# Down product in three passes with all four units through the ring, and Silu and Sigmoid as single activations

## The chip, the core and the metric

One core of one Trainium2 chip runs the kernel. The metric is the device time of one execution in microseconds (us). PE is the matrix engine, ACT the scalar engine with the activation functions, DVE the vector engine, POOL GpSimd, SP the engine whose queue issues most of the loads. The profile shows one execution of the kernel, taken by the hardware profiler.

## What is computed

The program is one inference step of a transformer trunk in float32: 512 new prompt tokens and 8 x 16 sample tokens, 640 rows of width 1024. As `DEPTH` is 1, it has one layer: a stick-breaking attention (16 heads of 64), and behind it a mixture of experts. The change lies in the second. Cut to what matters:

```python
def _grouped_moe(h, router_w, router_bias, w_gate, w_up, w_down):
    s = jax.nn.sigmoid((t @ router_w).astype(jnp.float32))
    sel = (s + router_bias.astype(jnp.float32)).reshape(-1, N_GROUPS, EXPERTS_PER_GROUP)
...
    for e in range(N_EXPERTS):
        he = jax.nn.silu(t @ w_gate[e]) * (t @ w_up[e])
        out = out + gates[:, e:e + 1] * (he @ w_down[e])
```

There are 16 experts in four groups; each token goes to two experts of one group. `w_gate` and `w_up` are 1024 x 512 for an expert, `w_down` 512 x 1024.

## The kernel before

**Slots.** After attention and the router, each token's row is scattered to its two experts' places in DRAM (`slots_in`). Rows of one expert lie together, in slots of 128 rows. The slot loop goes over these slots: PE's, ACT's, DVE's and SP's instructions each have a loop of their own, `Fori(1, m + 1)` on the three that compute (PE, ACT, DVE), and they meet through semaphores. In the runs shown m is 16, so there are 16 rounds; 18 slots in all, of which the first and the last two are partly or wholly outside the loop.

**Three passes of rounded halves.** A product of two float32 matrices is made with three matmuls. Each operand is split into a rounded half, `hi` (type fp32r, made by an ACT `Copy`), and the rest, `lo` (the raw value less `hi`, made by a DVE subtraction); PE adds hi·hi, hi·lo and lo·hi in one accumulation (`acc`, L1184). For the weights, a unit is 128 x 1024 values: `hi_unit` (L533, its instruction L535) writes `w_hi`, `lo_unit` (L537, L539) writes `w_lo`. Both are rings of `RING` = 4 units. A unit's place in the ring comes free when PE has used the unit that was there, which PE tells by `unit_used`; DVE tells PE by `lo_ready` that a unit is whole. A gate or an up matrix is four units, a down matrix too, but of the down matrix only the first `KS` = 3 go through the ring. Its fourth quarter goes to PE as it lies in memory, unrounded (`split_out`, the second `for k`). So a slot has `WUNITS` = 11 units. `units_before(j)` is the count of units ahead of slot j's gate.

**One round, by engine.** The order is written out by hand, and each engine goes through its list.
- PE (`phase_b_pe`, the loop at its end): `half_in(j, 0)`, the gate product, 24 matmuls; `turn_hid(j - 1)` and `next_slot(j)`, transposes of the last slot's hidden rows and of the next slot's x (L1282); `half_in(j, 1)`, the up product, 24; `split_out(j)`, the down product of slot j - 1, 18 in three passes and 2 x 1 unrounded (4 instructions).
- ACT: a `Sigmoid` of a 128 x 1 dummy (L790); `this_up(j)`, four units and the sigmoid of the gate product (L744); `last_down(j)`, the rounded half of `hidT` (L751) and three down units; `next_x_hi(j)` (L761); `next_gate(j)`, four units of the next slot's gate; `keep_y(j - 1)`, which copies the down product out of PE's accumulators (L779) and issues its store to `slots_out` (L782). Before units of a new matrix ACT looks up in a table (`slot_expert`, `slot_fetched`, L543 and L546) which of two buffers holds the expert's weights and how many loads must have landed.
- DVE: four up units; `keep_split_hidT`, a copy of the last quarter of `hidT` (L1018) and the rest of three quarters (L1019); `gate_by_sig`, the sigmoid times the gate product, which makes silu (L1030); three down units; `keep_hid` (L1036); `keep_slotT` (L996), the rest of the next slot's x; four gate units of the next slot.
- SP: the load of the next expert's gate, of the next slot's x, of the up, and of the down weights (L516), each when its buffer is free. The three weight loads are 2 MB each, double-buffered by the expert's parity, and left out when the next slot has the same expert. The down load waits for `down_ready`, which PE signals behind the unrounded quarter. The last down load is made in two parts (`load_down`, L518).

The copy `keep_y` waits for `down_ready` too. The gate units in `next_gate` wait for the down units whose places they take, the fourth for the third down unit, `min(u + 1, KS)`. The last two slots' down products (`out(m)` and `out(m + 1)`) are unrounded matmuls.

**Router.** ACT makes exp(-x) of the logits (L706), DVE adds 1 (L900) and takes the reciprocal (L901), and adds the bias (L902).

**End.** Behind the loop the last two slots are finished, while POOL gathers finished rows of `slots_out` and DVE weighs and adds them (L1069).

Of the kernel before, what the change touches and what calls it, by code (L numbers as in the profile page):

```python
# [17 lines left out]
P = 128  # L18
D = 1024
# [31 lines left out]
def build(nc, io, ctx):  # L51
# [163 lines left out]
    sb("h2_tok_end", [P, NT * D - 2 * D - 2 * FE - KF * P - NT * P])  # L215
# [4 lines left out]
    KS = 3  # L220
    WUNITS = 2 * RING + KS
# [23 lines left out]

    hidT_hi = nc.alloc_sbuf_tensor_at("hidT_hi", [P, KS, P], F32R, offset=tmp_at, align_bytes=32)
    hidT_lo = nc.alloc_sbuf_tensor_at("hidT_lo", [P, KS, P], F32R, offset=tmp_at + 4 * KS * P, align_bytes=32)
# [100 lines left out]
    last_down_loaded = sem("last_down_loaded")  # L348
# [41 lines left out]
    sig_step = sem("sig_step")  # L390
# [28 lines left out]
    def phase_b_sync(sp):  # L419
# [55 lines left out]
        with sp.Fori(1, m) as j:  # L475
# [6 lines left out]
            sp.wait_ge(down_ready, j)  # L482
            sp.nop(nofuse=True)
# [5 lines left out]
        sp.wait_ge(lo_ready, units_before(m) + 2 * RING + KS)  # L489
        sp.nop(nofuse=True)  # L490
        sp.wait_ge(exp_loaded[2], 16 * (m + 1))
        sp.nop(nofuse=True)
        load_down(sp, *before, range(0, KS), exp_loaded[2])
        sp.wait_ge(down_ready, m)
        sp.nop(nofuse=True)
        load_down(sp, *before, range(KS, KF), last_down_loaded)
# [21 lines left out]
    def load_down(sp, e, cond, ks, done):  # L518

        dst = exp_w[:, bass.ds(e % 2, 1), 8192 + ks[0] * D:8192 + ks[0] * D + len(ks) * D].rearrange("p b (k f) -> p b k f", f=D)  # L520
        src = io["exp_w_down"][0].rearrange("e (p k) f -> p e k f", p=P)
        sp.dma_start(dst, src[:, bass.ds(e, 1), ks[0]:ks[0] + len(ks)], cond=cond).then_inc(done, 16)

    def units_before(j):


        return 0 if isinstance(j, int) and j == 0 else j * WUNITS - KS
# [115 lines left out]
    def phase_b_act(act):  # L643
# [62 lines left out]
        act.activation(s_e[:, :, :], fill_ps[:, 0, 0:NT * NE].rearrange("p (t e) -> p t e", e=NE), ACT.Exp,  # L706
                       scale=-1.0).then_inc(sig_exp, 1)
# [20 lines left out]
        def this_up(j):  # L728
# [15 lines left out]
            act.activation(sig[:, :], zb(0), ACT.Sigmoid).then_inc(gate_sig, 1)  # L744

        def last_down(j):
# [17 lines left out]
        def next_gate(j, us=range(RING)):  # L764
# [31 lines left out]
        act.wait_ge(table_set, m + 2)  # L796
        act.activation(zero_a[:, :], eps1[:, :], ACT.Sigmoid).then_inc(table_set, 1)
        b = slot_expert(act, m + 1) % 2
        act.wait_ge(exp_loaded[1], slot_fetched(act, m + 1))
        for u in range(RING):  # L800
            act.wait_ge(unit_used, units_before(m + 1) + u + 1)
            hi_unit(act, b, RING + u)
            if u == 1:
                keep_y(m)
        act.wait_ge(unit_used, units_before(m + 1) + RING)
        act.wait_ge(hid_ready, m + 2)
        act.activation(sig[:, :], zb(0), ACT.Sigmoid).then_inc(gate_sig, 1)
        act.wait_ge(pick_turned, 1)
        act.activation(last_pick_T[:, :], turned_pick, ACT.Copy).then_inc(pick_kept, 1)
        act.wait_ge(table_set, m + 3)  # L810
# [1238 lines left out]
```

## Time and profile before

| what | value |
|---|---|
| median of 3 runs | 837.45 us (837.45, 835.5, 837.93) |
| profiled execution, its span | 832.8 us, 13544 instructions |
| PE busy | 775.9 us (93%) |
| PE weight loads busy (beside PE) | 585.2 us (70%) |
| DVE busy | 576.6 us (69%) |
| ACT busy | 480.0 us (58%) |
| POOL busy | 102.3 us (12%) |
| HBM, read and written | 272 GB/s over the span |

The span reaches from the first to the last instruction of the one execution that was profiled; of that execution the page gives the span and no other time. The times of the runs are device times of other executions, which the profiler didn't watch. The busy shares are means over the whole span; attention, the router and the slot loop have limits of their own, and the loop runs from some 487 us to 764 us of the span.

### The profile page before, as it was taken

The page shows a single profiled execution, that of the slowest core. Times are in us where ns is not written, and L with a number is a line of the kernel's source. Part 1 is how long each engine was busy: PE and PEld are TensorE (multiplying, and loading weights), DVE is VectorE, ACT ScalarE, POOL GpSimd, SP SyncE. Part 2 cuts the span into 40 slices and gives each one's busy share as a digit, 9 for nine tenths or more (in the row PEclk, how much of TensorE's full clock was granted, in tenths as well). Part 3 has the DMA queues.
Part 4 walks back from the last instruction along what each step waited for, and adds up shares of the span by engine and source line. Part 5 has one row for each costly group of instructions (what it writes and reads, how often), then busy time and mean ns, then how long its engine had stood idle before and what let it go on. Part 6 is the DMA issues. An engine that isn't in the chain of part 4 may idle for free.

```text
span 832.8 us, 13544 instructions
## 1 busy us (share of the span) xinstructions
PE 775.9 (93%) x4196; PEld 585.2 (70%) x4197; DVE 576.6 (69%) x720; ACT 480.0 (58%) x540; POOL 102.3 (12%) x165
## 2 busy tenths in 40 slices
PE   2799999999999999689997899999999999999987
PEld 0477878777787878458873577787777777877642
DVE  1375555647474655675567798788888887888697
ACT  5334553645453546571434577777777777777513
POOL 3000202011111112021001670000000000000150
PEclk9989999999999999989997999999999999999999
DMA  8937193939576684541009889758999999998563
GB/s 317 347 122 250 36 338 116 350 100 323 129 280 184 225 232 178 205 157 30 1 20 409 345 361 369 295 198 321 371 391 390 399 407 385 388 395 353 198 206 152
DMA packets 94971, 213.85 MB, mean 257 GB/s; under 512 B 4634, under 2 KB 55898, under 8 KB 88803
## 3 DMA queue, kind: packets, MB, share of 16 engines
q1 hardware_dynamic: 89620, 194.16, 64.3%
q0 software_dynamic: 2880, 10.49, 3.5%
q10 hardware_dynamic: 2448, 8.91, 2.6%
q8 instruction: 13, 0.21, 0.1%
q14 instruction: 10, 0.08, 0.0%
HBM read 181.56 MB, written 44.56 MB: 272 GB/s over the span
## 4 chain that ended last, share of the span: by engine, by line
PE 80%; DVE 7%; DMA 6%; ACT 3%; issue 2%; SPq 2%; POOL 1%; ACTq 0%; DVEq 0%; POOLq 0%
PE z L1184 38%; PE fill_ps L1911 18%; PE z L1911 11%; PE z L1148 5%; DMA ada_w<-in_ada_w 2%; PE z L1282 2%; PE fill_ps L1828 2%; DMA ada_w<-in_sb_w_o 2%; PE fill_ps L1184 1%; SPq L1445 1%; PE fill_ps L1834 1%; PE fill_ps L1315 1%; DVE w_lo L539 1%; DMA w_pair<-in_sb_w_qkv 1%; DVE h_T L1673 1%
## 5 line engine op out<-in xcount | busy, mean ns | idle before, releaser
L539 DVE TENSOR_TENSOR w_lo<-exp_w,w_hi 128x1024 fp32r<-128x1024 f32 x192 | 223.6, 1223 | 48.5 <-ACT w_hi L535 48.4
L535 ACT ACTIVATE w_hi<-exp_w 128x1024 fp32r (+1 forms) x192 | 196.4, 1055 | 57.1 <-PE z L1184 43.4
L1184 PE MATMUL z<-w_hi,x_slotT_hi 128*128 128x512 f32 x288 | 121.9, 423 | 2.8 <-ACT x_slotT_hi L761 1.3
L1184 PE MATMUL z<-w_lo,x_slotT_hi 128*128 128x512 f32 x288 | 113.4, 394 | 0.0
L1184 PE MATMUL z<-w_hi,x_slotT_lo 128*128 128x512 f32 x288 | 90.7, 396 | 0.1
L1911 PE MATMUL fill_ps<-h_hi,wp_hi 128*128 128x512 f32 x192 | 77.8, 405 | 1.7 <-DVE h_lo L1679 1.7
L1911 PE MATMUL fill_ps<-h_lo,wp_hi 128*128 128x512 f32 x192 | 77.1, 401 | 0.0
L1911 PE MATMUL fill_ps<-h_hi,wp_lo 128*128 128x512 f32 x192 | 76.6, 399 | 0.0
L1184 PEld LDWEIGHTS z<-w_hi,x_slotT_hi 128*128 128x128 f32 x288 | 54.2, 188 | 19.3 <-issue 3.8
L1184 PEld LDWEIGHTS z<-w_lo,x_slotT_hi 128*128 128x128 f32 x288 | 54.2, 188 | 14.9 <-issue 3.8
L1184 PEld LDWEIGHTS z<-w_hi,x_slotT_lo 128*128 128x128 f32 x288 | 53.9, 188 | 13.4 <-DVE x_slotT_lo L976 0.5
L1184 PE MATMUL z<-exp_w,hidT 128*128 x96 | 45.8, 611 | 1.0 <-DVE hidT L1025 1.0
L1828 PE MATMUL fill_ps<-ada_w,c_T 128*32 128x512 f32 x192 | 28.2, 714 | 19.5 <-DMA ada_w<-in_ada_w 18.5
L1911 PEld LDWEIGHTS fill_ps<-h_hi,wp_hi 128*128 128x128 f32 x192 | 36.6, 191 | 12.9 <-DVE h_lo L1679 3.2
L621 POOL DMA_INDIRECT exp_w<-slots_out,fetch_i x5 | 7.8, 1564 | 296.8 <-DVE w_lo L539 289.0
L1531 POOL TENSOR_SCALAR_AFFINE_SELECT ew_sp<-ew_sp 128x384 f32<-128x384 f32 (+3 forms) x32 | 14.1, 464 | 237.9 <-DVE ew_sp L1759 237.9
L1911 PEld LDWEIGHTS fill_ps<-h_hi,wp_lo 128*128 128x128 f32 x192 | 36.6, 191 | 8.5
L1911 PEld LDWEIGHTS fill_ps<-h_lo,wp_hi 128*128 128x128 f32 x192 | 36.7, 191 | 7.6
L1594 ACT ACTIVATE ew_t<-ew_t 128x1536 f32<-128x1536 f32 x16 | 23.8, 1488 | 31.5 <-DVE ew_t L1748 31.5
L1573 ACT ACTIVATE wp_hi<-w_pair 128x1024 fp32r<-128x1024 f32 x24 | 24.7, 1056 | 28.5 <-DMA w_pair<-in_sb_w_qkv 28.4
L1600 ACT ACTIVATE sp_hi<-ew_sp 128x1536 fp32r<-128x1536 f32 x16 | 23.8, 1489 | 29.8 <-POOL ew_sp L1546 19.0
L1184 PE MATMUL z<-w_hi,hidT_hi 128*128 128x512 f32 x96 | 38.2, 398 | 0.0
(349 smaller groups left out, 1499.6 us busy)
## 6 DMA issues: line engine op xcount, KB each, us to landing
exp_w<-in_exp_w_gate SPq DMA_DIRECT2D x18, 2048.0 KB
exp_w<-in_exp_w_up SPq DMA_DIRECT2D x18, 2048.0 KB
exp_w<-in_exp_w_down SPq DMA_DIRECT2D x17, 2048.0 KB
ada_w<-in_ada_w SPq DMA_DIRECT2D x12, 2048.0 KB, 10.1
slots_in<-zeros SPq DMA_DIRECT2D x7, 2048.0 KB, 12.8
w_pair<-in_sb_w_qkv SPq DMA_DIRECT2D x24, 512.0 KB, 5.3
slots_out<-y_slot ACTq DMA_DIRECT2D x17, 512.0 KB, 10.4
x_slot<-slots_in SPq DMA_DIRECT2D x16, 512.0 KB, 9.3
```

The lines of the kernel that those rows point to most:

```text
L535: act.activation(w_hi[:, u % RING, :].unsqueeze(1), raw_unit(b, u), ACT.Copy).then_inc(hi_ready, 1)
L539: dve.tensor_tensor(w_lo[:, u % RING, :].unsqueeze(1), raw_unit(b, u), w_hi[:, u % RING, :].bitcast(F32).unsqueeze(1), ALU.subtract).then_ ...
L1148: return pe.matmul(proj_ps(q), lhsT, rhs, start=start, stop=stop, skip_group_check=True)
L1184: return pe.matmul(out, lhsT, rhs, start=start, stop=stop, skip_group_check=True)
L1282: mm = pe.transpose(z[:, 2048 + k * P:2048 + (k + 1) * P], src[:, :].rearrange("p (c k) -> p k c", k=KD)[:, k, :], ident[:, :])
L1315: mm = pe.transpose(fill_ps[:, 0, k * P:(k + 1) * P], hid[:, :].rearrange("p (c k) -> p k c", k=KF)[:, k, :], ident[:, :])
L1531: last = pool.affine_select(out=v, in_=v, compare_op=ALU.is_gt, fill=0.0, base=0, pattern=[[0, n], [1, P]] if n > 1 else [[1, P]], channel ...
L1573: act.activation(wp_hi[:, c], w_pair[:, c], ACT.Copy).then_inc(wp_hi_ready, 1)
L1594: act.activation(ew_t[:, a], ew_t[:, a], ACT.Exp, scale=-1.0).then_inc(exp_ready, 1)
L1600: act.activation(sp_hi[:, a], ew_sp[:, a], ACT.Copy).then_inc(sp_hi_ready, 1)
L1828: mm = pe.matmul(out[CW * g:CW * g + CW, :], c_T[:, k, :], src[:, k, :], start=(k < NG4), stop=(k >= NG4), skip_group_check=True)
L1911: return pe.matmul(out, lhsT, rhs, start=start, stop=stop, skip_group_check=True)
```

## The change

The fourth quarter of the down matrix goes through the ring as well: `KS` is gone, `WUNITS` is 12, `hidT_hi` and `hidT_lo` hold all four quarters, and the down product has 24 matmuls of the three-pass kind and no unrounded one. The fourth gate unit on ACT waits for the fourth down unit in place of the third, and `keep_y` waits for `unit_used` of that unit, with `down_ready` left to the last two slots. The load of the next down weights on SP waits for `lo_ready` of the fourth unit, in place of PE's `down_ready`; the last one is a single load. `Silu` on ACT takes the place of the sigmoid and DVE's product (`gate_by_sig`), `Sigmoid` in the router that of exp, the addition and the reciprocal. The dummy activations go, but for one that asks for `Sigmoid` ahead of the router; `preload_act_table` asks for Silu's table ahead of the loop and for Sqrt's at the end.

```diff
     RING = 4
     UK = KD // RING
-    KS = 3
-    WUNITS = 2 * RING + KS
+    WUNITS = 3 * RING
...
@@ SP's loop
             sp.wait_ge(lo_ready, units_before(j) + 2 * RING)
             fetch_over(1, j, *now)
-            sp.wait_ge(down_ready, j)
-            sp.nop(nofuse=True)
+            sp.wait_ge(lo_ready, units_before(j) + 3 * RING)
             fetch_over(2, j - 1, *before)
         before = next_of(m, -1)
-        sp.wait_ge(lo_ready, units_before(m) + 2 * RING + KS)
...
-        load_down(sp, *before, range(KS, KF), last_down_loaded)
+        sp.wait_ge(lo_ready, units_before(m) + 3 * RING)
+        fetch_over(2, m - 1, *before)
...
@@ ACT, router
-        act.activation(zero_a[:, :], eps1[:, :], ACT.Exp).then_inc(table_set, 1)
+        act.activation(zero_a[:, :], eps1[:, :], ACT.Sigmoid).then_inc(table_set, 1)
...
-        act.activation(s_e[:, :, :], fill_ps[:, 0, 0:NT * NE].rearrange("p (t e) -> p t e", e=NE), ACT.Exp,
-                       scale=-1.0).then_inc(sig_exp, 1)
+        act.activation(s_e[:, :, :], fill_ps[:, 0, 0:NT * NE].rearrange("p (t e) -> p t e", e=NE),
+                       ACT.Sigmoid).then_inc(sig_exp, 1)
...
         m = act.value_load(slot_tab[0:1, TAB_N:TAB_N + 1], min_val=NE - 2, max_val=MAX_SLOTS - 2)
+        act.preload_act_table(ACT.Silu)
         act.wait_ge(table_set, 1)
-        act.activation(zero_a[:, :], eps1[:, :], ACT.Sigmoid).then_inc(table_set, 1)
-        act.wait_ge(table_set, 2)
...
@@ ACT, slot loop
-            act.activation(sig[:, :], zb(0), ACT.Sigmoid).then_inc(gate_sig, 1)
+            act.activation(sig[:, :], zb(0), ACT.Silu).then_inc(gate_sig, 1)
...
-            act.activation(hidT_hi[:, :, :], fill_ps[:, 0, 0:KS * P].rearrange("p (k c) -> p k c", c=P),
+            act.activation(hidT_hi[:, :, :], fill_ps[:, 0, :].rearrange("p (k c) -> p k c", c=P),
                            ACT.Copy).then_inc(hidT_hi_ready, 1)
-            for u in range(KS):
+            for u in range(RING):
                 act.wait_ge(unit_used, units_before(j) + RING + u + 1)
                 hi_unit(act, b, 2 * RING + u)
...
-                    act.wait_ge(unit_used, units_before(j) + 2 * RING + min(u + 1, KS))
+                    act.wait_ge(unit_used, units_before(j) + 2 * RING + u + 1)
                 hi_unit(act, b, u)
-        def keep_y(j):
-            act.wait_ge(down_ready, j + 1)
+        def keep_y(j, last=False):
+            if last:
+                act.wait_ge(down_ready, 1)
+            else:
+                act.wait_ge(unit_used, units_before(j + 1) + 3 * RING)
             act.wait_ge(y_slot_stored, 16 * (j + 1))
...
         with act.Fori(1, m + 1) as j:
-            act.wait_ge(table_set, j + 1)
-            act.activation(zero_a[:, :], eps1[:, :], ACT.Sigmoid).then_inc(table_set, 1)
             this_up(j)
...
@@ DVE
-        step(dve.tensor_scalar_add(s_e[:, :, :], s_e[:, :, :], 1.0))
-        step(dve.reciprocal(s_e[:, :, :], s_e[:, :, :]))
...
-            dve.tensor_copy(hidT[:, KS:KF, :], whole[:, KS:KF, :])
-            dve.tensor_tensor(hidT_lo[:, :, :], whole[:, 0:KS, :], hidT_hi[:, :, :].bitcast(F32),
-                              ALU.subtract).then_inc(hidT_kept, 1)
+            dve.tensor_tensor(hidT_lo[:, :, :], fill_ps[:, 0, :].rearrange("p (k c) -> p k c", c=P),
+                              hidT_hi[:, :, :].bitcast(F32), ALU.subtract).then_inc(hidT_kept, 1)
...
             keep_split_hidT(j - 1)
-            gate_by_sig(j)
-            rest_of_down(j, range(KS))
+            rest_of_down(j, range(RING))
             keep_hid(j)
...
@@ PE, split_out
-            b = slot_expert(pe, j - 1) % 2
-            pe.wait_ge(exp_loaded[2], slot_fetched(pe, j - 1))
             pe.wait_ge(y_slot_kept, j)
             pe.wait_ge(hidT_kept, j)
-            for k in range(KS):
+            for k in range(KF):
...
-            for k in range(KS, KF):
-                for c in range(2):
-                    mm = acc(zb(2 + c), hidT[:, k, :],
-                             exp_w[:, bass.ds(b, 1), 8192 + k * D + c * 512:8192 + k * D + (c + 1) * 512], stop=(k == KF - 1))
-            mm.then_inc(down_ready, 1)
...
-            pe.wait_ge(sig_step, j)
+            pe.wait_ge(gate_sig, j)
```

How this moves the instructions is shown at three places, as each engine has them in its program; words in brackets are semaphores that an instruction waits for, ISA and REGISTER_ALU rows are waits and register work.

On PE, the end of the down product in the slot loop (`split_out`), before:

```order
L1184 MATMUL z<-w_hi,hidT_hi 128x512 [waits lo_ready]
L1184 MATMUL z<-w_lo,hidT_hi 128x512
L1184 MATMUL z<-w_hi,hidT_lo 128x512
L1184 MATMUL z<-w_hi,hidT_hi 128x512
L1184 MATMUL z<-w_lo,hidT_hi 128x512
L1184 MATMUL z<-w_hi,hidT_lo 128x512
L1184 ISA
L1184 MATMUL z<-exp_w,hidT 128x512
L1184 ISA
L1184 MATMUL z<-exp_w,hidT 128x512
L1365 ISA
L1365 COMPARE_AND_BRANCH
```

and with the change, from the same third unit on:

```order
L1153 MATMUL z<-w_hi,hidT_hi 128x512
L1153 MATMUL z<-w_lo,hidT_hi 128x512
L1153 MATMUL z<-w_hi,hidT_lo 128x512
L1297 REGISTER_ALU
L1153 MATMUL z<-w_hi,hidT_hi 128x512 [waits lo_ready]
L1153 MATMUL z<-w_lo,hidT_hi 128x512
L1153 MATMUL z<-w_hi,hidT_lo 128x512
L1153 MATMUL z<-w_hi,hidT_hi 128x512
L1153 MATMUL z<-w_lo,hidT_hi 128x512
L1153 MATMUL z<-w_hi,hidT_lo 128x512
L1327 ISA
L1327 COMPARE_AND_BRANCH
```

Behind the third unit the unrounded matmuls on `exp_w` have given way to six matmuls on the ring's fourth unit, with a wait for `lo_ready` of their own.

On ACT, the end of a round, from the third gate unit to the loop's branch, before:

```order
L772 REGISTER_ALU
L535 ISA [waits unit_used]
L535 ACTIVATE w_hi<-exp_w 128x1024
L535 ISA [waits unit_used]
L535 ACTIVATE w_hi<-exp_w 128x1024
L778 REGISTER_ALU [waits down_ready]
L779 ACTIVATE y_slot<-z 128x1024 [waits y_slot_stored]
L782 ISA [waits y_slot_kept]
L782 DMA slots_out<-y_slot 128x1024
L788 ISA
L788 COMPARE_AND_BRANCH
```

and with the change:

```order
L755 REGISTER_ALU
L519 ISA [waits unit_used]
L519 ACTIVATE w_hi<-exp_w 128x1024
L755 REGISTER_ALU
L519 ISA [waits unit_used]
L519 ACTIVATE w_hi<-exp_w 128x1024
L764 REGISTER_ALU [waits unit_used]
L765 ACTIVATE y_slot<-z 128x1024 [waits y_slot_stored]
L768 ISA [waits y_slot_kept]
L768 DMA slots_out<-y_slot 128x1024
L774 ISA
L774 COMPARE_AND_BRANCH
```

A register addition now stands ahead of the fourth gate unit, as that unit waits for a later count of `unit_used` than the third; and the copy of y waits for `unit_used` where `down_ready` stood.

On ACT, the top of the loop, between the branch and the first up unit, before:

```order
L788 UNCONDITIONAL_BRANCH
L788 ISA
L790 ACTIVATE zero_a<-eps 128x1 [waits table_set]
L543 ISA
L543 TENSOR_LOAD slot_tab
L543 ISA x2
L546 ISA
L546 TENSOR_LOAD slot_tab
L546 ISA x2
L737 ISA [waits up_loaded]
```

and with the change:

```order
L774 UNCONDITIONAL_BRANCH
L774 ISA
L527 TENSOR_LOAD slot_tab
L527 ISA x2
L530 ISA
L530 TENSOR_LOAD slot_tab
L530 ISA x2
L720 ISA [waits up_loaded]
```

The dummy activation with its wait is gone, and the two lookups in `slot_tab` follow the branch at once.

## Rows read from the trace of the kernel before

**Rows 1.** The page: its span, and the group of hi·hi matmuls in the down product.

```profile
span 832.8 us, 13544 instructions
...
L1184 PE MATMUL z<-w_hi,hidT_hi 128*128 128x512 f32 x96 | 38.2, 398 | 0.0
```

**Rows 2.** One round by windows: window, PE, PEld, DVE, ACT, POOL busy, clock, DMA, GB/s.

```profile
644.96:663.40 18.44, 18.44 (x83) 14.46 (x83) 15.43 (x17) 14.10 (x17) 0.00 (x0) 1.00 0.97 393
```

**Rows 3.** The chain of waits, transposes of the next slot (start, us, what).

```profile
523.46 0.90 PE z L1282 x8
542.22 0.90 PE z L1282 x8
560.66 0.90 PE z L1282 x8
```

**Rows 4.** Timeline of PE, 657 to 673: start, us, line, operation, tiles, count [idle before].

```profile
659.50 0.40 PE L1184 MATMUL z<-w_hi,hidT_hi 128*128 128x512 f32 x1
...
663.47 0.40 PE L1184 MATMUL z<-w_hi,hidT_lo 128*128 128x512 f32 x1
663.71 1.88 PE L1184 MATMUL z<-exp_w,hidT 128*128 x4
...
665.65 0.40 PE L1184 MATMUL z<-w_lo,x_slotT_hi 128*128 128x512 f32 x1
...
672.29 0.47 PE L1184 MATMUL z<-w_hi,x_slotT_hi 128*128 128x512 f32 x1
```

**Rows 5.** The timeline of ACT in the same stretch.

```profile
663.99 2.01 ACT L535 ACTIVATE w_hi<-exp_w 128x1024 fp32r x2 [0.34 <-PE z L1184]
665.91 1.01 ACT L779 ACTIVATE y_slot<-z 128x1024 f32<-128x1024 f32 x1
...
667.83 0.20 ACT L790 ACTIVATE zero_a<-eps 128x1 f32<-128x1 f32 x1 [0.92 <-ACT y_slot L779]
669.32 3.90 ACT L535 ACTIVATE w_hi<-exp_w 128x1024 fp32r x4 [1.29 <-DMA exp_w<-in_exp_w_up]
```

**Rows 6.** The timeline of DVE in the same stretch.

```profile
657.52 0.68 DVE L1030 TENSOR_TENSOR sig<-sig,z 128x512 f32<-128x512 f32 x1
658.11 3.49 DVE L539 TENSOR_TENSOR w_lo<-exp_w,w_hi 128x1024 fp32r<-128x1024 f32 x3
...
663.25 4.63 DVE L539 TENSOR_TENSOR w_lo<-exp_w,w_hi 128x1024 fp32r<-128x1024 f32 x4
670.61 3.50 DVE L539 TENSOR_TENSOR w_lo<-exp_w,w_hi 128x1024 fp32r<-128x1024 f32 x3 [2.73 <-ACT w_hi L535]
```

**Rows 7.** The timeline of all engines, 573 to 580 us, in one of two longer rounds.

```profile
573.38 1.00 ACT L779 ACTIVATE y_slot<-z 128x1024 f32<-128x1024 f32 x1
...
577.27 3.90 ACT L535 ACTIVATE w_hi<-exp_w 128x1024 fp32r x4 [1.77 <-PE z L1184]
...
578.56 4.63 DVE L539 TENSOR_TENSOR w_lo<-exp_w,w_hi 128x1024 fp32r<-128x1024 f32 x4 [3.35 <-ACT w_hi L535]
...
579.84 0.50 PE L1184 MATMUL z<-w_hi,x_slotT_hi 128*128 128x512 f32 x1
```

**Rows 8.** The timeline of SP's queue, 645 to 650 us.

```profile
647.73 0.34 SPq L516 DMA_DIRECT2D exp_w<-in_exp_w_down  x1
```

**Rows 9.** The timeline of DVE at the router, 443 to 447 us.

```profile
444.13 0.20 DVE L900 TENSOR_SCALAR s_e<-s_e 128x80 f32<-128x80 f32 x1 [3.30 <-ACT s_e L706]
...
445.05 0.24 DVE L902 TENSOR_TENSOR sel<-s_e,router_b 128x80 f32<-128x80 f32 x1
```

**Rows 10.** The timeline of all engines behind the slot loop, from 776 us.

```profile
776.55 1.01 ACT L779 ACTIVATE y_slot<-z 128x1024 f32<-128x1024 f32 x1
...
788.99 1.28 DVE L1069 SCALAR_TENSOR_TENSOR exp_w<-exp_w,gates,gate 128x1024 f32<-128x1024 f32 x1 [4.55 <-DMA exp_w<-slots_out,fetch_i]
...
795.39 0.68 DVE L1036 TENSOR_TENSOR hid<-sig,z 128x512 f32<-128x512 f32 x1
```

**Rows 11.** Groups of instructions by line, tables of ACT in attention (busy us, mean ns).

```profile
L1597 ACT ACT_TABLE_LOAD x8 | 10.3, 1283 | 0.1
```

More of the change, by code:

```diff
@@ L214, in build @@
     last_pick_T = sb("last_pick_T", [P, NT * P])
-    sb("h2_tok_end", [P, NT * D - 2 * D - 2 * FE - KF * P - NT * P])
+    hidT_lo = sb("hidT_lo", [P, KF, P], F32R)
+    sb("h2_tok_end", [P, NT * D - 2 * D - 2 * FE - 2 * KF * P - NT * P])
     x_slotT_hi = sb("x_slotT_hi", [P, KD, P], F32R)
@@ L244, in build @@
     g_ffn = tmp
-    hidT_hi = nc.alloc_sbuf_tensor_at("hidT_hi", [P, KS, P], F32R, offset=tmp_at, align_bytes=32)
-    hidT_lo = nc.alloc_sbuf_tensor_at("hidT_lo", [P, KS, P], F32R, offset=tmp_at + 4 * KS * P, align_bytes=32)
+    hidT_hi = nc.alloc_sbuf_tensor_at("hidT_hi", [P, KF, P], F32R, offset=tmp_at, align_bytes=32)
     ZIN = -(-(MAX_SLOTS + 1) // (NPAIR - 1))
@@ L389, in build @@
     gate_sig = sem("gate_sig")
-    sig_step = sem("sig_step")
     hid_ready = sem("hid_ready")
@@ L481, in phase_b_sync @@
             fetch_over(1, j, *now)
-            sp.wait_ge(down_ready, j)
-            sp.nop(nofuse=True)
+            sp.wait_ge(lo_ready, units_before(j) + 3 * RING)
             fetch_over(2, j - 1, *before)
         before = next_of(m, -1)
-        sp.wait_ge(lo_ready, units_before(m) + 2 * RING + KS)
[L490 to L495, printed above, removed]
-        load_down(sp, *before, range(KS, KF), last_down_loaded)
+        sp.wait_ge(lo_ready, units_before(m) + 3 * RING)
+        fetch_over(2, m - 1, *before)
         sp.wait_ge(x_slot_loaded, 16 * m)
@@ L516, in load_expert @@
         sp.dma_start(dst, src[:, bass.ds(e, 1)], **more).then_inc(exp_loaded[i], 16)
[L518 to L522, printed above, removed]
     def units_before(j):
-        return 0 if isinstance(j, int) and j == 0 else j * WUNITS - KS
+        return 0 if isinstance(j, int) and j == 0 else j * WUNITS - RING
     def raw_unit(b, u):
@@ L795, in phase_b_act @@
             keep_y(j - 1)
-        act.wait_ge(table_set, m + 2)
-        act.activation(zero_a[:, :], eps1[:, :], ACT.Sigmoid).then_inc(table_set, 1)
         b = slot_expert(act, m + 1) % 2
@@ L803, in phase_b_act @@
             if u == 1:
-                keep_y(m)
+                keep_y(m, last=True)
         act.wait_ge(unit_used, units_before(m + 1) + RING)
         act.wait_ge(hid_ready, m + 2)
-        act.activation(sig[:, :], zb(0), ACT.Sigmoid).then_inc(gate_sig, 1)
+        act.activation(sig[:, :], zb(0), ACT.Silu).then_inc(gate_sig, 1)
         act.wait_ge(pick_turned, 1)
         act.activation(last_pick_T[:, :], turned_pick, ACT.Copy).then_inc(pick_kept, 1)
-        act.wait_ge(table_set, m + 3)
-        act.activation(zero_a[:, :], eps1[:, :], ACT.Sqrt).then_inc(table_set, 1)
-        act.wait_ge(down_ready, m + 2)
+        act.preload_act_table(ACT.Sqrt)
+        act.wait_ge(down_ready, 2)
         act.wait_ge(y_slot_stored, 16 * (m + 2))
@@ L1014, in keep_split_hidT @@
         def keep_split_hidT(j):
-            whole = fill_ps[:, 0, :].rearrange("p (k c) -> p k c", c=P)
             dve.wait_ge(hidT_hi_ready, j + 1)
-            dve.tensor_copy(hidT[:, KS:KF, :], whole[:, KS:KF, :])
-            dve.tensor_tensor(hidT_lo[:, :, :], whole[:, 0:KS, :], hidT_hi[:, :, :].bitcast(F32),
-                              ALU.subtract).then_inc(hidT_kept, 1)
+            dve.tensor_tensor(hidT_lo[:, :, :], fill_ps[:, 0, :].rearrange("p (k c) -> p k c", c=P),
+                              hidT_hi[:, :, :].bitcast(F32), ALU.subtract).then_inc(hidT_kept, 1)
         def keep_hidT(j):
@@ L1025, in keep_hidT, with keep_hid @@
             dve.tensor_copy(hidT[:, :, :], fill_ps[:, 0, :].rearrange("p (k c) -> p k c", c=P)).then_inc(hidT_kept, 1)
-        def gate_by_sig(j):
+        def keep_hid(j):
             dve.wait_ge(gate_sig, j + 1)
-            dve.tensor_tensor(sig[:, :], sig[:, :], zb(0), ALU.mult).then_inc(sig_step, 1)
-        def keep_hid(j):
-            dve.wait_ge(sig_step, j + 1)
             dve.wait_ge(unit_used, units_before(j) + 2 * RING)
@@ L1108, in phase_b_dve @@
         dve.wait_ge(x_slot_loaded, 16 * m)
-        dve.wait_ge(down_ready, m + 2)
+        dve.wait_ge(down_ready, 2)
         for c in range(2):
@@ L1334, in split_out @@
                     acc(zb(2 + c), hidT_hi[:, k, :], w_lo[:, k, cols])
-                    mm = acc(zb(2 + c), hidT_lo[:, k, :], w_hi[:, k, cols])
+                    mm = acc(zb(2 + c), hidT_lo[:, k, :], w_hi[:, k, cols], stop=(k == KF - 1))
                 mm.then_inc(unit_used, 1)
-            for k in range(KS, KF):
-                for c in range(2):
-                    mm = acc(zb(2 + c), hidT[:, k, :],
-                             exp_w[:, bass.ds(b, 1), 8192 + k * D + c * 512:8192 + k * D + (c + 1) * 512], stop=(k == KF - 1))
-            mm.then_inc(down_ready, 1)
         def out(j):
@@ L1384, in phase_b_pe @@
         turn_hid(m + 1)
-        pe.wait_ge(last_down_loaded, 16)
         out(m + 1)
```

3 lines of the change are left out of this document (removed).

## The prediction, made before the changed kernel ran

> **What bounds the kernel now.** I read the page first (its span and its groups), then the table by stages, the chain of waits, and the timeline of one round, engine by engine. A round is one turn of the slot loop; PE's three-pass matmuls of the down product come in 96, six for each of three units, so there are 16 rounds [rows 1]. In a round's stretch PE is busy 18.44 of 18.44 us, and the DMA engines are near full as well, share 0.97 [rows 2]. The chain of waits is PE alone through the loop: from one turn of a slot to the next it takes 18.44 us, and 18.76 in two of the rounds [rows 3]. So a round costs what its matmuls cost, as long as ACT and DVE deliver each unit in time. How near they are to being late is read from the timeline. I count from T, the moment at which PE starts the next slot's gate product. The second gate matmul starts at 665.65 and matmuls of this kind stand 0.234 apart (18 of them from 659.50 to 663.71 [rows 4]), so T = 665.42. PE starts the up product at 672.29, T + 6.87 [rows 4]. Its first unit comes by this path: ACT copies y (665.91, T + 0.49), issues its store, branches, looks up two table entries, rounds the first up unit from 669.32, 3.41 after the start of the copy [rows 5]; DVE subtracts from 670.61 for 1.22 us (three take 3.50, so they stand 1.14 apart) [rows 6]. That is 671.83, 0.46 before PE needs it. In a longer round the copy is 3.89 from the unit, and PE starts 0.06 after DVE's end [rows 7]. So ACT has less than half a microsecond to spare where the slots meet.
>
> **The matmuls.** The fourth quarter of the down product takes PE from 663.71 to T, 1.71 us, as unrounded matmuls [rows 4]. Three passes of two column halves are six matmuls at 0.234, 1.40 us. PE saves 0.31 us a round, 5.0 over 16 rounds. A page of the Trainium skill, TensorE: Matmul & The Clock Gate, section "Wait — 56ns, not 53.3ns?", gives about 216 ns from one warm 512-column matmul to the next; by it the six would take 1.30 and the saving would be 6.6 us. The rows show 0.234, and they decide.
>
> **The wait that it brings.** The down product now uses all four places of the ring, so the last gate unit can't be rounded until PE has used the fourth down unit, at T. Before, its place was free with the third, and ACT did it under the unrounded matmuls (it ends the pair that starts at 663.99, and y follows 0.95 after its start, at 665.91 [rows 5]). ACT answers a used unit quickly: the last three-pass matmul starts at 663.47 and lasts 0.40, so ends at 663.87 [rows 4]; ACT starts at 663.99, 0.12 later [rows 5]. With the last matmul now starting at T − 0.23 and ending at T + 0.17, ACT starts that unit at T + 0.29, and y at T + 1.24 in place of T + 0.49. Behind y on ACT are its store, the branch and the up unit. The change takes the little activation at the loop's top away (667.83 [rows 5]). What that gives lies between nothing and the 0.20 that it lasts; I take 0.05, nearer nothing, since ACT idles 0.92 before it and 1.29 behind it: the path runs through the lookups, not through it. So the up unit starts at T + 1.24 + 3.36 = T + 4.60, DVE 1.29 later as now [rows 5, 6], and its end, 1.22 + 0.06 later [rows 6, 7], is T + 7.17. PE could start at T + 6.87. It waits 0.30 us a round, in the 15 rounds that follow a y copy. The gain of 0.31 is given back but for 0.01; only the first round keeps it whole: **−0.5 us for the typical rounds**.
>
> Two rounds now cost 0.31 too much, by lookups that make 3.41 into 3.89 [rows 3, 7]. If they come back, each costs its whole 0.48, 0.34 more for the two together; if they don't, the kernel gains 0.6. SP's own lookups, which follow its issue of the down weights (647.73 [rows 8]), move ahead with it, away from ACT's; but no row proves that the two disturb each other. I take zero, between −0.6 and +0.8 (the other rounds' lookups vary too).
>
> **DVE.** It loses the product with sig (0.59 to the next start [rows 6]) and a small copy, and gains the subtraction of a unit, 1.14, and a quarter of hidT_lo. Its four gate units end at 663.25 + 4.63 = 667.88, and it idles from there to 670.61, 2.7 us [rows 6]: that covers the net half a microsecond. Its order matters once: the rest of x and the first gate unit now stand behind one more unit. Counted from the first up unit at T + 5.89 in steps of 1.14 (four up units, four down), 0.6 twice (hidT_lo and hid) and 1.14 (x), the first gate unit starts at T + 17.35 and ends at T + 18.57, and the next T is at 7.17 + (18.44 − 6.87 − 0.31) = T + 18.43. PE may start its gate product 0.2 late; the up product would then be ready for PE at 0.2 + 6.87 = 7.07 after the next T, still before its first unit at 7.17. Nothing is added.
>
> **The down weights' load** waits for the last subtraction, not for PE: the fourth down unit ends at about T + 15.7, 2.7 before the next T, where the issue now comes 0.75 after T (647.73, against 665.42 − 18.44 = 646.98) [rows 3, 8]. Some 3.5 us earlier, then, for weights that are used a round and more later, so it is worth nothing. That the loads are near full [rows 2] doesn't bind a round that stays at 18.4.
>
> **The router.** Sigmoid on ACT spares DVE an addition and a reciprocal, from 444.13 to 445.05 [rows 9], with PE, the scatter and the first slot behind them: −0.92. The activation itself takes ACT no longer as far as its size goes; a bound for that is nothing to 0.2.
>
> **The end.** The next to last y copy comes 0.75 later, and so do its store and the gather for which DVE waits until 788.99; from there DVE works through to hid at 795.39 [rows 10]. It has the product with sig less (0.59). So hid, PE's last transposes and the last down product come 0.15 later: +0.15, with 0 and 0.75 as the ends.
>
> **Sum.** −0.5 + 0 − 0.92 + 0.15 = −1.3. The profiled execution's span is 832.8 [rows 1]; it becomes 831.5. The median of the three runs is 4.65 above that span, and with the same around it the time is 837.45 − 1.3 = 836.1, say **836.0 us**. That is 0.17% less; a measurement of this kernel can tell about 0.3%, 2.5 us, from no change (834.9 to 840.0).
>
> **The rivals.**
> *PE's gain comes through.* If ACT is not late (the fourth unit's place is seen earlier than I count, or the path from y to the unit is 0.3 shorter), the rounds give 5.0, the two longer ones 0.6, and the router 0.9: 831.0. For it: 0.3 us is all that it needs, and half of it gives 833.5. Against: each piece of the path is a row, and they repeat in the two rounds that I compared (1.29 in both [rows 5 to 7]). Chance 0.18.
> *ACT's path grows: slower.* Place: the stretch between the y copy and the first up unit. Each 0.1 us there costs PE 0.1 in each of 15 rounds, 1.5 us, since no slack is left. From 0.27 us a round on, the kernel is slower than 840.0. If every round is like the longer ones, 3.89 for 3.41 [rows 7], it is 15 × 0.48 = 7.2: 843.2. For it: such rounds are there. Against: two of 15. Chance 0.12.
> *A table load in each round.* Silu is used in the loop, rounded copies are too; if each turn had to load a table, 1.28 us [rows 11] would stand on ACT's path in each of 15 rounds: 836.0 + 19.2 = 855. The order of the changed kernel has one load ahead of the loop and none in it, so I give it 0.02. The page of the Trainium skill on ScalarE activation tables: per-element evaluation and per-set limits, section "Table sets in the compiler and the runtime", says that the back end places the loads block by block, by which a loop's body might get one of its own; by that rule a load could stand there, and the trace of before shows none in the round of rows 5, which has a function with a table too.
>
> **How the numbers follow.** The forecast, ACT's wait in the place of PE's saving, has 0.68, with a range of its own of 834 to 838.5: −0.6 to +0.8 for the lookups, 0 to +0.6 at the end, 0.05 to 0.2 for the dropped activation (up to −2), and runs that differ by 2 us among themselves. Some 0.16 of it falls below 834.9 and almost none above 840. Faster: 0.18 + 0.16 = 0.34. Slower: 0.12 + 0.02 = 0.14. No change that can be told: 0.52. A range of 831.0 to 839.5 leaves out the lower half of the first rival (0.09) and nearly all of the slower cases.
>
> **What would show it.** In the profile after: 24 three-pass matmuls and no unrounded one in a round; the last gate unit on ACT 0.3 after T and y 0.95 behind it; PE's first up matmul at about T + 7.17, with an idle or stretched stretch of 0.3 put down to DVE's w_lo; rounds of 18.4 as before. PE's busy share in the loop, now full, should fall to about 98%. I am wrong if the rounds shrink to 18.13 (ACT is in time), or if they grow past 18.7 (its path is longer). Each other step has its row: no addition and no reciprocal ahead of sel, and no product with sig on DVE.

## The result and the profile after

The changed kernel takes 840.85 us (median of 8 runs, 837.88 to 844.1); the kernel before, run beside it, 835.92 (8 runs, 834.83 to 837.93). The ratio is 1.0059, 95% interval 1.0044 to 1.0075: **slower by 0.6%, 4.9 us**, where I had forecast no change that can be told, and outside my range. It is the rival that I gave 0.12: ACT's path between the copy of y and the first up unit has grown.

The page after: its span, busy times and the three groups of the down product's matmuls.

```profile
span 841.0 us, 13498 instructions
...
PE 776.6 (92%) x4228; PEld 591.4 (70%) x4229; DVE 582.6 (69%) x700; ACT 488.8 (58%) x537; POOL 96.1 (11%) x165
...
L1153 PE MATMUL z<-w_hi,hidT_lo 128*128 128x512 f32 x128 | 50.7, 396 | 0.0
L1153 PE MATMUL z<-w_hi,hidT_hi 128*128 128x512 f32 x128 | 50.7, 396 | 0.0
L1153 PE MATMUL z<-w_lo,hidT_hi 128*128 128x512 f32 x128 | 50.4, 394 | 0.0
...
slots_out<-y_slot ACTq DMA_DIRECT2D x17, 512.0 KB, 6.5
```

The 128 in place of 96 [rows 1] are the fourth unit's matmuls. The last line is the store of y, 6.5 us from issue to landing. The same line of the page before:

```profile
slots_out<-y_slot ACTq DMA_DIRECT2D x17, 512.0 KB, 10.4
```

The store lands sooner now, and that turns out to be the story.

The table by stages, a stretch of 277 us inside the slot loop, of the kernel before and, below it, of the changed one (columns as in [rows 2]):

```profile
487.00:764.00 277.00, 277.00 (x1230) 217.64 (x1229) 232.14 (x240) 211.69 (x240) 7.79 (x6) 1.00 0.91 364
```

```profile
487.00:764.00 277.00, 272.41 (x1236) 218.51 (x1235) 235.09 (x220) 216.68 (x235) 1.92 (x2) 1.00 0.93 362
```

PE had no gap in this stretch; now it has 4.6 us of gaps, at the same granted clock. From the first up product in the loop to the last, 15 rounds, it is 277.24 before and 284.15 after (starts of PE's matmuls): 6.9 us, more than the whole loss.

The chain of waits of the changed kernel where two slots meet, from the copy of y to PE's first up matmul. "ACTq" is ACT's sequencer; L527 and L530 are the two lookups in `slot_tab`, L768 the issue of y's store, "issue" small gaps:

```profile
671.20 1.02 ACT y_slot L765
...
672.42 0.35 ACTq L768
...
673.12 0.27 ACTq L527
...
673.73 0.67 ACTq L530
...
674.91 1.07 ACT w_hi L519
...
676.20 1.24 DVE w_lo L523
...
677.48 0.74 PE z L1153 x2
```

The chain that ran through PE alone before [rows 3] now goes, in nearly every round, through ACT's copy, store, lookups and first up unit, and through DVE. One link is longer than it was: the second lookup, 0.67 us. The view of the instructions that read `slot_tab` has their duration (min/median/max, ns). The same stretch of the kernel before (from 665.9, the copy of rows 5) and of the changed one:

```profile
L543 ACTq TENSOR_LOAD <-slot_tab x1: 287/287/287, 667.9 to 667.9; - x1
L546 ACTq TENSOR_LOAD <-slot_tab x1: 278/278/278, 668.5 to 668.5; - x1
```

```profile
L527 ACTq TENSOR_LOAD <-slot_tab x1: 274/274/274, 673.1 to 673.1; - x1
L530 ACTq TENSOR_LOAD <-slot_tab x1: 669/669/669, 673.7 to 673.7; - x1
```

I went through the 15 rounds that follow a y copy. Before, the second lookup is never over 0.45 us and the first twice, in the two longer rounds. After, the second is over 0.45 in 13 rounds, up to 1.15, the first in 5. From copy to first up unit it is 3.51 on the mean before and 3.86 after.

What differs around them is the order of two transfers. SP issued the down load 0.3 us after the copy's start in the kernel before, with y's store 0.9 behind it; it now issues it 3.5 us ahead of the copy (667.75 against 671.20), 4.7 ahead of the store. The first packets on ACT's queue then move 3.0 to 3.8 us after the copy's start in most rounds, where it had been 4.6 to 5.4. The issues of the down load and of the next gate load, first in the kernel before, then in the changed one:

```profile
666.17 0.34 SPq L516 DMA_DIRECT2D exp_w<-in_exp_w_down  x1
671.22 0.34 SPq L516 DMA_DIRECT2D exp_w<-in_exp_w_gate  x1
```

```profile
667.75 0.34 SPq L506 DMA_DIRECT2D exp_w<-in_exp_w_down  x1
674.02 0.34 SPq L506 DMA_DIRECT2D exp_w<-in_exp_w_gate  x1
```

The two longer rounds of the kernel before fit: the next slot had the same expert, so the down load was left out (its issue is a row of 0.09 us there), next to nothing stood ahead of the store (the up load landed 0.4 to 0.9 after the store's issue), its packets moved 2.1 after the copy, both lookups were longer (0.65 and 0.40, 0.63 and 0.42), and the up unit came 3.89 after the copy [rows 7]. So **theory A**: lookups take long when y's store is being started, and the early down load no longer holds the store back. **Theory B**: the lookups' place alone, 0.08 earlier since the dummy activation is gone.

### The profile page after: what moved, and what is told of

It is laid out like the page before. It is cut to its first block, busy times and chain, and to the rows that moved or that the text cites. A ratio compares the mean times of both kernels' runs of the same rounds, so it can differ in the third digit from the quotient of the medians.

```text
span 841.0 us, 13498 instructions
## 1 busy us (share of the span) xinstructions
PE 776.6 (92%) x4228; PEld 591.4 (70%) x4229; DVE 582.6 (69%) x700; ACT 488.8 (58%) x537; POOL 96.1 (11%) x165
## 4 chain that ended last, share of the span: by engine, by line
PE 70%; DVE 8%; ACT 6%; issue 5%; DMA 4%; ACTq 4%; POOL 2%; SPq 2%; DVEq 0%; POOLq 0%
PE z L1153 29%; PE fill_ps L1872 18%; PE z L1872 11%; PE z L1117 5%; DMA ada_w<-in_ada_w 2%; DVE w_lo L523 2%; ACT w_hi L519 2%; PE fill_ps L1789 2%; ACTq L530 2%; ACT y_slot L765 2%; PE fill_ps L1117 1%; PE fill_ps L1153 1%; SPq L1406 1%; PE fill_ps L1795 1%; POOL slots_in L556 1%
## 5 line engine op out<-in xcount | busy, mean ns | idle before, releaser
L523 DVE TENSOR_TENSOR w_lo<-exp_w,w_hi 128x1024 fp32r<-128x1024 f32 x208 | 241.7, 1223 | 50.6 <-ACT w_hi L519 50.2
L519 ACT ACTIVATE w_hi<-exp_w 128x1024 fp32r (+1 forms) x208 | 211.8, 1055 | 73.0 <-PE z L1153 64.1
L1153 PE MATMUL z<-w_hi,x_slotT_hi 128*128 128x512 f32 x288 | 117.7, 409 | 8.0 <-DVE w_lo L523 5.4
L1153 PE MATMUL z<-w_hi,hidT_lo 128*128 128x512 f32 x128 | 50.7, 396 | 0.0
L1153 PE MATMUL z<-w_hi,hidT_hi 128*128 128x512 f32 x128 | 50.7, 396 | 0.0
L1153 PE MATMUL z<-w_lo,hidT_hi 128*128 128x512 f32 x128 | 50.4, 394 | 0.0
L1789 PE MATMUL fill_ps<-ada_w,c_T 128*32 128x512 f32 x192 | 26.5, 675 | 21.3 <-DMA ada_w<-in_ada_w 20.3
```

The lines of the kernel that those rows point to most:

```text
L519: act.activation(w_hi[:, u % RING, :].unsqueeze(1), raw_unit(b, u), ACT.Copy).then_inc(hi_ready, 1)
L523: dve.tensor_tensor(w_lo[:, u % RING, :].unsqueeze(1), raw_unit(b, u), w_hi[:, u % RING, :].bitcast(F32).unsqueeze(1), ALU.subtract).then_ ...
L1153: return pe.matmul(out, lhsT, rhs, start=start, stop=stop, skip_group_check=True)
L1789: mm = pe.matmul(out[CW * g:CW * g + CW, :], c_T[:, k, :], src[:, k, :], start=(k < NG4), stop=(k >= NG4), skip_group_check=True)
```

## The experiments

**1. The down load back behind PE, in the changed kernel.**

```diff
-            sp.wait_ge(lo_ready, units_before(j) + 3 * RING)
+            sp.wait_ge(unit_used, units_before(j) + 3 * RING)
             fetch_over(2, j - 1, *before)
```

> One line of the changed kernel goes back in kind: SP's load of the next down weights waits until PE has used the fourth down unit (as before), not for the fourth subtraction. Theory A (the order of two transfers): in the changed kernel the down load is issued 3.5 us before the y copy, so nothing stands ahead of y's store, which starts 3.0 to 3.7 us after the copy's start in place of 4.6 to 5.4, and ACT's second table lookup takes 0.4 to 1.0 us in place of 0.28. With the down load back at 0.3 us after the copy, the lookups take 0.28 again, the first up unit comes 3.32 after the copy (3.84 on the mean now), rounds are 18.4 (18.9 now) and the time is about 833 to 835. Theory B (the loop's top): the lookups are longer because the dummy activation ahead of them is gone and they come 0.08 earlier; then nothing changes here: lookups to 1.0, rounds of 18.9, 840.9.

835.96 us, 0.9996 of the kernel before (0.9981 to 1.001): A, though not the 833 to 835 that I expected of it. One wait is the whole loss. The load is now issued 0.54 ahead of the copy and 1.7 ahead of the store, not 0.3 behind the copy as I wrote. Both of ACT's lookups of a round and a lookup of SP's, again from the view by tile:

```profile
L451 SPq TENSOR_LOAD <-slot_tab x2: 262/268/273, 669.8 to 671.6; - x2
L527 ACTq TENSOR_LOAD <-slot_tab x1: 282/282/282, 670.9 to 670.9; - x1
L530 ACTq TENSOR_LOAD <-slot_tab x1: 277/277/277, 671.5 to 671.5; - x1
```

SP's second (671.6) falls on ACT's second, and neither is long, so it is not lookups that hold each other up. Twelve rounds have such lookups (the second takes 0.28 to 0.38), and are 18.39 to 18.50 long (from one up product to the next). The three others are those in which no down load stands ahead of the store: the first, in which it is issued behind it (8.17 from T to the up product in place of 6.87), and the two with the same expert (18.94 and 18.97). That is why it is no better than the kernel before: its 15 rounds take 278.73, 1.5 more than before, and 1.1 of that is in the first.

**2. The dummy activation back.**

```diff
         with act.Fori(1, m + 1) as j:
+            act.wait_ge(table_set, j)
+            act.activation(zero_a[:, :], eps1[:, :], ACT.Silu).then_inc(table_set, 1)
             this_up(j)
```

> The changed kernel with a 128x1 dummy activation (Silu) and its wait at the top of ACT's loop again. Theory A: no better; the second lookup stays at 0.4 to 1.0 us, rounds 18.9 or 0.1 more, 841 to 842. Theory B: the lookups come as late as in the kernel before and take 0.28 each, the first up unit comes 3.41 after the copy, rounds 18.5, some 834 to 835.

843.48 us (1.0086, 1.0067 to 1.0106). The second lookup is over 0.45 in 12 of 15 rounds, the unit comes 3.92 after the copy. B falls.

**3. The copy of y ahead of the fourth gate unit.**

```diff
             act.activation(y_slot[:, :], z[:, 1024:2048], ACT.Copy).then_inc(y_slot_kept, 1)
+            if behind is not None:
+                hi_unit(act, behind, RING - 1)
             act.wait_ge(y_slot_kept, j + 2)
...
-            next_gate(j)
-            keep_y(j - 1)
+            b = next_gate(j, range(RING - 1))
+            keep_y(j - 1, behind=b)
```

> The changed kernel, but on ACT the copy of y is put ahead of the fourth gate unit, which then runs while the store is issued and the lookups are made; both waited for the same signal of PE. If the chain y copy, store, lookups, first up unit is what sets the rounds (both theories of the lookups, and my reading of the trace after), it begins 0.97 earlier: the first up unit is whole at T + 6.4 (by 3.84 from copy to unit) where PE wants it at T + 6.87, and rounds fall from 18.9 to PE's own 18.14, the time to 828 to 831. Rival: DVE's chain or the loads (7.3 MB a round, 405 GB/s at 18.14) set the rounds as well; then they stay at 18.4 or more and the time at 833 or above.

832.09 us (0.995, 0.9932 to 0.9968), between the two: of fifteen rounds nine are 18.25 to 18.30, three 18.36 to 18.39, three 18.61 to 18.72. The path from the copy does set the rounds. The timeline of ACT in a short one:

```profile
664.69 1.03 ACT L766 ACTIVATE y_slot<-z 128x1024 f32<-128x1024 f32 x1 [0.33 <-PE z L1156]
665.61 1.04 ACT L519 ACTIVATE w_hi<-exp_w 128x1024 fp32r x1
665.92 0.35 ACTq L771 DMA_DIRECT2D slots_out<-y_slot  x1
668.44 2.01 ACT L519 ACTIVATE w_hi<-exp_w 128x1024 fp32r x2 [1.78 <-PE z L1156]
```

The store is issued while the gate unit (665.61) runs, and the unit no longer stands ahead of the copy, so its 0.96 is off the path. The lookups come as late behind the copy as in the changed kernel and are still long, DVE's too when it looks up at the same time:

```profile
L527 DVEq TENSOR_LOAD <-slot_tab x1: 705/705/705, 667.2 to 667.2; - x1
L530 ACTq TENSOR_LOAD <-slot_tab x1: 669/669/669, 667.3 to 667.3; - x1
```

Two engines are held up and let go together, so it is no matter of ACT's own.

**4 and 8. The kernel before with a later down load.** Two tries at the converse, to make the kernel before lose in the same way.

```diff
             sp.wait_ge(down_ready, j)
             sp.nop(nofuse=True)
+            sp.wait_ge(y_slot_stored, 16 * (j + 1))
+            sp.nop(nofuse=True)
             fetch_over(2, j - 1, *before)
```

> The kernel before with one wait more on SP: the down load is issued only when y's store has landed, so that the store has no load of the same round ahead of it. Theory A: y's store starts within 2 to 4 us of the copy in every round as it did in the two longer rounds (in which no down load was issued, its expert being there), ACT's lookups take 0.4 to 0.7 in place of 0.28, the up unit is 0.05 late and a round costs 18.7 to 18.8: 13 rounds by 0.32, some 839 to 840. Theory B: no lookup gets longer, rounds of 18.44, 835.9.

863.06 us (1.0314, 1.0285 to 1.0343), for another reason: SP, held up by the store, issues the next loads too late, and PE waits for the next slot's x. The view of waits, 600 to 800 us (us in total, times, longest):

```profile
PE z L1284 <- DMA x_slot<-slots_in: 17.6, 4, 5.2
```

The time tells nothing of A. The trace agrees with it in the two rounds in which no weight load was moving when the store was issued: the first lookup takes 0.70 and 0.65 there. In the second try, SP waits for the next slot's first up unit:

```diff
-            sp.wait_ge(down_ready, j)
+            sp.wait_ge(lo_ready, units_before(j + 1) + RING + 1)
             sp.nop(nofuse=True)
             fetch_over(2, j - 1, *before)
```

> The kernel before with one wait changed: SP issues the down load when the first up unit of the next slot is whole (some 6 us later than now), a cleaner form of the late load than waiting for the store. Theory A: nothing stands ahead of y's store, it starts 2 to 3.7 us after the copy's start, the lookups take 0.4 to 1.0, the first up unit comes 3.8 to 3.9 after the copy as in the two longer rounds, and rounds are 18.6 to 18.8: 838 to 840. If SP's later gate load makes weights late instead, rounds are longer and the wait is on the load. Otherwise: lookups 0.28, 18.44, 836.0.

836.89 us (1.0024, 1.0008 to 1.0039), and nearly all rounds as before: 18.44, lookups of 0.28. My expectation missed, and the trace says why: gate, x and up loads were now issued together (623.57 to 624.85 in one round), 5.6 us ahead of the copy, and were still queued; the store's packets began 4.6 to 5.2 after the copy all the same, but for the first round and the one without a load, in which the first lookup takes 0.70 and 0.65. By these rounds it is not the time of an issue that counts but how much is still queued ahead of the store.

**5. The store behind the first up unit.** ACT's loop is turned, so that copy, lookups, unit and store stand in one body.

```diff
                 hi_unit(act, b, RING + u)
+                if u == 0 and stored is not None:
+                    store_y(stored)
...
+        with act.Fori(1, m) as j:
+            last_down(j)
+            next_x_hi(j)
+            next_gate(j)
+            keep_y(j - 1)
+            this_up(j + 1, stored=j - 1)
```

> The changed kernel, down load early as in it, but ACT issues y's store behind the first up unit of the next slot (its loop is turned so that copy, lookups, unit and store stand in one body); nothing is left out. Theory A, sharpened: it is the store under way that makes the lookups long, not the down load under way. Then the two lookups, now made before the store is issued, take 0.28 each in every round, and the first up unit starts at the copy's end or 0.5 behind it, 1.0 to 1.5 after its start in place of 3.84; PE is never late for the up product and rounds are 18.14 to 18.3: 828 to 831. Theory A2: it is the load (early, and under way at that time): the lookups stay at 0.5 to 1.0; the time gains all the same, since the path is shorter by the store's issue and the branch.

831.68 us (0.9953, 0.994 to 0.9965); every round is 18.25 to 18.27, and all 30 lookups between copy and up unit take 0.27 to 0.29. But they also come 2.8 us earlier, so earlier in the down load's course; that is left to number 9.

**6. Numbers 1 and 3 together.**

```diff
-            sp.wait_ge(lo_ready, units_before(j) + 3 * RING)
+            sp.wait_ge(unit_used, units_before(j) + 3 * RING)
...
-            next_gate(j)
-            keep_y(j - 1)
+            b = next_gate(j, range(RING - 1))
+            keep_y(j - 1, behind=b)
```

> The copy ahead of the fourth gate unit and the down load behind PE's last use, both. Theory A: with the load ahead of the store again the lookups take 0.28, the rounds of 18.6 to 18.7 that the copy alone still had go to 18.25, and the time is 1 to 2 us under that kernel's 832.1: 830 to 831. If the loads bind by now (share 0.99 at 406 GB/s in a round of 18.25), the later issue costs and it is 832 or more.

830.38 us, 0.9942 of the kernel before (0.9929 to 0.9955): A's figure. All rounds are 18.25 to 18.27, also the four that have a lookup over 0.45, as the path has room for it. The loads run at 421 GB/s, share 1.00, in one such round (643.72 to 661.99) and don't bind yet:

```profile
643.72:661.99 18.27, 18.27 (x85) 14.82 (x85) 16.50 (x16) 14.96 (x16) 0.00 (x0) 1.00 1.00 421
```

**7. The activations alone, in the kernel before.**

```diff
-            act.activation(sig[:, :], zb(0), ACT.Sigmoid).then_inc(gate_sig, 1)
+            act.activation(sig[:, :], zb(0), ACT.Silu).then_inc(gate_sig, 1)
...
-            act.wait_ge(table_set, j + 1)
-            act.activation(zero_a[:, :], eps1[:, :], ACT.Sigmoid).then_inc(table_set, 1)
...
-        step(dve.tensor_scalar_add(s_e[:, :, :], s_e[:, :, :], 1.0))
-        step(dve.reciprocal(s_e[:, :, :], s_e[:, :, :]))
...
-            gate_by_sig(j)
```

> The kernel before with the activations alone: Silu, Sigmoid in the router, no dummy activations; the down product keeps its unrounded quarter, the down load its place. My sum says -0.92 for the router, nothing for the loop (PE's rounds stay 18.44) and up to -0.6 at the end: 834.5 to 835.2. Rival: the router's gain is hidden by the scatter, and it is 836.0 as before.

833.2 us (0.9969, 0.9957 to 0.9981): faster by 2.7, not by 0.9 to 1.5. The router's part is as reckoned: from the start of ACT's activation to that of `sel` it is 1.26 before (443.79 to 445.05 [rows 9]) and 0.34 here, as in the changed kernel, whose timeline at the router has:

```profile
445.04 0.24 ACT L690 ACTIVATE s_e<-fill_ps 128x80 f32<-128x80 f32 x1 [0.70 <-PE fill_ps L1153]
...
445.38 0.24 DVE L881 TENSOR_TENSOR sel<-s_e,router_b 128x80 f32<-128x80 f32 x1 [3.25 <-ACT s_e L690]
```

How much of these 0.92 is left behind the router no profile tells: from `sel` to the first up product in the loop it is 41.9 to 44.3 us in the twelve profiles. The loop gives 0.26 (276.98 for 277.24), the end 1.0 (67.3 from the start of the last up product for 68.3). The same stretch at the end is 67.7 to 69.9 in the profiles of the other kernels, without a pattern that I can name, so a single profile doesn't tell what the rest of the 2.7 is.

**9. Number 5 with the lookups at their old time.** A wait for the copy and three waited dummy activations stand ahead of the lookups:

```diff
+            act.wait_ge(y_slot_kept, j + 2)
+            act.nop(nofuse=True)
+            for i in range(3):
+                act.activation(zero_a[:, :], eps1[:, :], ACT.Copy).then_inc(table_set, 1)
+                act.wait_ge(table_set, 3 * k + 2 + i)
+                act.nop(nofuse=True)
```

> The kernel with the store behind the first up unit, with a wait for the copy and three waited dummy activations put ahead of the lookups, so that they come about as late after the copy's start as in the changed kernel (1.7 to 2.0 us), in the same part of the down load's landing, but with no store issued before them. Theory A (the store must have been issued): both lookups take 0.28 in every round, the first up unit comes 3.0 to 3.3 after the copy, rounds 18.25 to 18.4, 831.5 to 834. Rival (the load's course alone): the second lookup takes 0.6 to 1.0 again, the unit comes 3.6 to 4.0 after the copy, rounds 18.7 to 18.9, 838 to 841.

833.07 us (0.9962, 0.9946 to 0.9979). The second lookup starts 2.50 after the copy, 6.0 after the down load's issue, as in the changed kernel (2.53 and 6.0), and of 30 lookups none is over 0.30:

```profile
L527 ACTq TENSOR_LOAD <-slot_tab x1: 278/278/278, 666.9 to 666.9; - x1
L530 ACTq TENSOR_LOAD <-slot_tab x1: 278/278/278, 667.5 to 667.5; - x1
```

Same load, same moment, no store issued yet: short. The rounds are 18.37 to 18.42, but for the first (18.91). So a long lookup needs the store's issue, and with numbers 1 and 2 theory A is shown. What it is in the store's start that holds a lookup up is not shown.

**10. Number 6 with DVE's first gate unit ahead of the rest of x.**

```diff
             keep_hid(j)
+            rest_of_gate(j + 1, range(1))
             keep_slotT(j + 1)
-            rest_of_gate(j + 1)
+            rest_of_gate(j + 1, range(1, RING))
```

> The fastest so far (copy first, down load behind PE's last use), and on DVE the first gate unit ahead of the rest of x. In a round of 18.25, PE still loses 0.04 at the slot's first matmul to DVE's first gate unit and 0.10 in restarting behind it; the rest of x is wanted only four matmuls later. Expected: rounds of 18.14, 15 by 0.11, so 828.5 to 829.5 against 830.4. Rival: one more lookup on DVE a round costs as much, and it stays at 830 to 831.

830.53 us (0.993, 0.9902 to 0.9959): the rounds are 18.20, 0.05 shorter, which the time can't tell from number 6.

## Why the prediction was wrong

- **The down weights' load** is the step that failed. I put its move at "worth nothing", since the weights have a round to spare, and never asked which transfer would no longer be held up by it. It costs 4.9 us (840.85 against 835.96 with that wait alone put back; in the 15 rounds of the two profiles 284.15 against 278.73, 5.4).
- **The lookups.** "SP's own lookups ... move ahead with it, away from ACT's ... I take zero" was wrong in its cause. SP's lookups did move away, and ACT's path from the copy to the up unit got longer, by 0.35 on the mean in each of 15 rounds, 5.2 us: its two lookups together take 1.09 on the mean for 0.66, and the dummy activation gives 0.09 back. The two longer rounds [rows 3, 7] held the answer: they are the ones without a down load. I looked for a meeting of lookups, and did not ask what else was missing.
- **ACT's path grows**, the rival, had the right place and price (each 0.1 us costs 1.5 us; 0.48 would give 843.2, and the 0.35 measured 841.2), but a chance of 0.12: I took "two of 15" for a frequency, where it was a condition that the change makes common.
- **The wait that the fourth unit brings** held, piece by piece. T was to be 0.234 behind the start of the down product's last matmul. Counted from there, the changed kernel's fourth gate unit starts at T + 0.29, as I had it, and y at T + 1.26 for 1.24. With the lookups short (number 1) the up product starts at T + 7.14 to 7.24 for 7.17, and a round is 18.39 to 18.50 for 18.43 to 18.44. Where PE loses the time differs: some 0.25 goes at the gate product, which waits for DVE's first gate unit (I allowed 0.2), and the rest at the up product.
- **The matmuls** held: where nothing else is late (numbers 5 and 6) rounds are 18.25, against 18.44; of the 0.31 reckoned, 0.12 goes at the first gate matmul, which waits for DVE's unit and restarts.
- **The first y copy** was to cost PE 0.30 like the others; its up product starts 8.16 behind the gate product for 6.87, 1.3 late, as no load stands ahead of its store and the lookups take 0.53 and 1.15.
- **A table load in each round** did not come: the changed kernel's loads at and behind the router start at 438.4, 463.4 and 800.2 us, none of them in the loop.
- **The router** held as far as `sel` (0.34 for 1.26, so -0.92); beyond it the profiles differ by more than that. **The end** (+0.15) can't be told among ends that differ by 2 us and more.
- **The base** was off: where a run's span and time are both known, the time is 1.73 to 1.86 above the span, not 4.65. The profiled execution was at the short end, and the median of three at the long end of runs whose median is 835.92. From there my -1.3 gives 834.6.

## What to carry to other kernels

When a transfer is moved, ask not only whether its own data come in time but which other transfer had been waiting behind it, and who shares a resource with that one. A few rounds of a loop that differ from the rest are an experiment already made: find what they lack before putting a cause on them. And where two instructions wait for the same signal, the one with a tail behind it goes first: that alone, an exchange of two lines, turned this loss into a gain of 0.5%, and with the old wait for the load into 0.6%.

## What the runs showed of the hardware

A lookup in the table takes some 0.28 us, and 0.5 to 1.45 when it falls into the start of y's store. In the nine profiles of the kernel before, the changed one and numbers 1 to 3 and 5 to 8, I sorted the 2058 lookups of all engines that start between 495 and 768 us. With no store issued in the 5.5 us before, one of 1229 is over 0.45; within 0.65 us of an issue none of 70. From 0.65 to 2.1 us after the store's issue it goes by the weight load that is moving: with fewer than 44 of its 128 packets landed 4 of 120 are over 0.45, with 44 to 95 landed 51 of 72, with more 21 of 134, and with no load moving 41 of 53. From 2.1 to 5.5 us after the issue it is 48 of 107 with 44 to 95 landed, and 5 of 273 otherwise. (I chose these bounds after seeing the lookups.)

So the kernel before has the long lookups too, in another place. Of its lookups in that stretch 17 are over 0.45, 18 in the changed kernel. Before, 2 of them are ACT's between copy and up unit, and 10 are of ACT's next pair, ahead of `last_down`, 4.3 us or more after the store's issue, where no wait of PE follows. After, 17 of the 18 are ACT's between copy and up unit. The first of that next pair in the kernel before, at 671.5, is the longer of the two in this line:

```profile
L543 ACTq TENSOR_LOAD <-slot_tab x2: 283/696/1108, 671.5 to 678.2; - x2
```

What fits is that an issued store is worked on only once the load ahead of it is well under way, and that lookups are held up then. The change did not make lookups long; it moved the store's start onto those that PE depends on. What exactly holds them up stays open: the long ones start between 2.8 us before (number 3) and 1.7 us after the store's first packet on record, and no run here separates the reading of `y_slot` from the store's set-up. The Trainium skill, DMA: Bandwidth & Descriptors, section "Queues, rings and completion order", says that each DMA engine takes turns between the queues that it has work for, packet by packet. By that a store on ACT's queue need not wait for a load on SP's; the traces agree only in part, as its first packet came 1.8 to 2.5 us after its issue in the rounds of the changed kernel that have a load under way, and 3.4 to 4.2 in those of the kernel before that have one just issued; with none moving it came 0.85 to 0.90 after.
